# A hybrid decoder layer on one core: blocks of the delta rule's inverse turned by VectorE, side work in other slots, convolution states turned four tiles at a time

## The chip, the core and the metric

The kernel runs on one core of a Trainium2 chip. A core has TensorE (PE: matmuls and their weight loads), VectorE (DVE), ScalarE (ACT), GpSimd (POOL) and SyncE (SP, which here only issues DMAs). They run side by side and wait for each other through semaphores. The metric is the device time of one execution in microseconds (us). Of the kernel before, three runs were timed: 2022.98, 2025.06 and 2025.74 us, median 2025.06 us.

## The reference, cut to what matters

One layer for a prompt (256 tokens) and 8 samples of 8 tokens, 320 columns in all, in float32:

```python
h = rms_norm(x); proj = h @ w_in        # -> u (S5) | q k v | z | beta | a | two gates
# branch A: S5, a diagonal complex state space model, 64 groups, scan over positions
y = gelu(Re(C h) + D u);  y = y * sigmoid(y @ w_glu + b_glu)
# branch B: causal convolution (width 4) over [buf | qkv], SiLU, l2-norm of q and k, gated delta rule
out = sum_j xp[:, j:j + L] * w[j];  conv_new = xp[:, L:]        # the convolution states go in and out
lower = where(strict, beta * (k k^T) * decay, 0)                # one 128x128 matrix for each head and chunk
tmat = triangular_solve(eye + lower, eye)                       # the inverse
u = tmat @ (v * beta);  w = tmat @ (k * beta * exp(gc))
# merge, output projection, SwiGLU FFN (5632), a gated input embedding, final norm
x = x + (sigmoid(ga) * (y_s5 @ w_a) + sigmoid(gb) * (y_dn @ w_b)) @ w_out
x = x + (silu(h2 @ w_gate) * (h2 @ w_up)) @ w_down
x = x + (p @ w_ple) * sigmoid(h3 @ w_ple_gate)
```

## The kernel before

**Units.** All large products are cut into units. A unit is four tiles of 128 rows of a weight by 256 columns, loaded by SP into `raw` (a ring of four). ScalarE rounds it to `whi` (`split_hi`, L931), VectorE takes the rest `wlo = raw - whi` (`split_lo`, L1384), and TensorE multiplies in three parts of eight matmuls: `whi` with the high part of the activations, `whi` with the low part, `wlo` with the high part (L2117). Four units (two in `glu`, `wa`, `wb`) make a pair of output tiles in PSUM (`pg`), which VectorE takes out (`evac`).

**Slots.** `schedule()` writes the order of the mixer by hand: a list of slots, each with a list of side work and a number of units. Within a slot TensorE does its side work first and then the units; VectorE, ScalarE and POOL do the slot's units first (their splits and evacuations) and then its side work. Every engine runs through its own instructions strictly in this order. Side products land in two PSUM regions, `side_a` and `side_b`; `side_fills()` lists in which order they are filled. A region is filled again when the one before was drained.

**Stages of the mixer**, with the time in the profile: x turned and the first norm (to 50 us); set-up of the S5 tables, a long chain on POOL (33 to 93 us); sixteen S5 slots (88 to 308 us), in which TensorE makes the drives (`drive`, L2465) before the last unit of an odd slot and the readouts (`readout`, L2481 to L2490) before the last unit of an even one, while VectorE works through `s5_tiles`; the tail, in which the last three columns of the convolution go out (`tail`, L2276; `tailc`, L1704); eight convolution slots (`conv`, L1716) with the small decay functions (`decay`, L1072 to L1078) put between them; l2 norms (`l2a`, `l2s`, `l2b`); the delta rule in three chunks of 128, 128 and 64 columns (426 to 700 us); the gate products `glu` with `late` (L1460 to L1462), and then `wa` and `wb`.

**The inverse.** `per_block` (L2160) multiplies the 32x32 blocks on the diagonal of each head. `tm` holds the inverse so far, `tmt` its transpose; at level k TensorE makes `m1 = ltm . tm` (side work `m1`), ScalarE copies it out, then TensorE makes `ta = tmt . m1` and `tb = m1 . tmt` (`tab`), and VectorE subtracts `ta` from `tm` (L1828) and `tb` from `tmt` (L1837). At level 0 a product with the identity gives the transpose of `ltm` (`ident,ltm`). Levels 5 and 6 join the blocks to larger ones. Chunks 0 and 1 have seven levels, chunk 2 has three.

## Time and profile before

| what | value |
|---|---|
| median of three runs | 2025.06 us |
| the profiled execution's own time | 2022.08 us |
| its span, first to last instruction | 2020.3 us |
| PE busy | 1997.2 us (99%), 16379 matmuls |
| DVE busy | 1117.8 us (55%) |
| ACT busy | 822.8 us (41%) |
| POOL busy | 295.0 us (15%) |
| chain that ended last | PE 93%, DVE 3%, ACT 2%, issue 1% |
| DMA | 154 GB/s mean |

The page also cuts the span into 40 slices of 50 us and gives the busy share in tenths: in slices 3 to 6 (100 to 300 us, the S5 stage) DVE reads 9, 9, 9, 8 and ACT 4, 3, 3, 3; in slices 7 and 8 (the tail and the convolution stage) ACT reads 6 and 8. Busy time of PE is not PE at its peak, since matmuls are pipelined and their ends are modelled; the time from the start of one group to the start of the next tells more. "issue" is idle time for which the profile shows no releaser. A timeline row gives the start, the time, engine, line, operation, output<-inputs, the count of merged instructions, and in brackets the idle time before it with what ended it. A float32 matmul stands as two instructions in the trace where the program has one.

### The profile page before, as it was taken

To read this page: it belongs to the slowest core of one execution; us is meant where nothing else is said; L and a number is where in the kernel's file an instruction comes from. 1 tells how busy PE (TensorE), PEld (TensorE's weight loads), DVE (VectorE), ACT (ScalarE), POOL (GpSimd) and SP (SyncE) were. 2 spreads that over 40 slices of the span, in tenths; PEclk is the share of its full clock that TensorE was granted. 3 is DMA by queue.
4 is the path that set the end of the run, shared out by engine and by line. 5 is a ranking of instruction groups with operands and counts; after the bars stand their busy time and mean duration, and the time that the engine had idled before them with its cause. 6 is when DMAs were issued, how large, how long until landed. Compare 5 with 4: busy or idle time off the path is not lost.

```text
span 2020.3 us, 40308 instructions
## 1 busy us (share of the span) xinstructions
PE 1997.2 (99%) x16379; PEld 1952.0 (97%) x16379; DVE 1117.8 (55%) x1401; ACT 822.8 (41%) x1076; POOL 295.0 (15%) x372
## 2 busy tenths in 40 slices
PE   9999999999999999999999999999999999999998
PEld 8999999899999879999999999999999999999998
DVE  6899987674535677644444444333444444444554
ACT  7343336843433455343433333333333333334543
POOL 3855532000002110011000000000000000011110
PEclk9999999999999999999999999999999999999999
DMA  8544444544345686744444444444544444444442
GB/s 200 182 137 147 126 136 143 148 120 138 111 122 166 187 250 214 238 151 150 146 147 154 146 148 155 146 151 146 156 145 149 152 146 151 145 147 152 150 146 100
DMA packets 299648, 310.26 MB, mean 154 GB/s; under 512 B 24771, under 2 KB 290068, under 8 KB 299220
## 3 DMA queue, kind: packets, MB, share of 16 engines
q1 hardware_dynamic: 295844, 296.76, 47.9%
q0 software_dynamic: 3264, 11.64, 2.1%
q8 instruction: 91, 1.49, 0.3%
q14 instruction: 31, 0.25, 0.0%
q10 hardware_dynamic: 418, 0.12, 0.0%
HBM read 291.34 MB, written 17.14 MB: 153 GB/s over the span
## 4 chain that ended last, share of the span: by engine, by line
PE 93%; DVE 3%; ACT 2%; issue 1%; DMA 0%; SPq 0%; ACTq 0%; DVEq 0%
PE pg L2117 86%; DVE cacc L1716 1%; PE side_a L2160 1%; DVE wlo L1384 1%; PE side_a L2151 1%; ACT whi L931 1%; PE side_b L2160 0%; PE side_a L2465 0%; PE side_a L2117 0%; DMA xtok<-in_x_sample 0%; PE side_b L2124 0%; PE side_a L2484 0%; PE side_b L2426 0%; PE side_b L2117 0%; ACT qkv L1002 0%
## 5 line engine op out<-in xcount | busy, mean ns | idle before, releaser
L1384 DVE TENSOR_TENSOR wlo<-raw,whi 128x1024 fp32r<-128x1024 f32 (+1 forms) x528 | 651.3, 1241 | 660.0 <-ACT whi L931 658.4
L931 ACT ACTIVATE whi<-raw 128x1024 fp32r<-128x1024 f32 (+1 forms) x528 | 545.3, 1039 | 910.3 <-PE pg L2117 867.1
L2117 PE MATMUL pg<-xhi,whi 128*128 128x320 f32 x2816 | 479.4, 312 | 2.5 <-ACT whi L931 2.5
L2117 PE MATMUL pg<-xhi,wlo 128*128 128x320 f32 x2816 | 470.6, 309 | 1.3 <-issue 1.2
L2117 PE MATMUL pg<-xlo,whi 128*128 128x320 f32 x2816 | 470.2, 309 | 0.0
L2117 PEld LDWEIGHTS pg<-xhi,whi 128*128 128x128 f32 x2816 | 424.7, 188 | 13.0 <-issue 6.7
L2117 PEld LDWEIGHTS pg<-xhi,wlo 128*128 128x128 f32 x2816 | 427.3, 188 | 0.5 <-DVE wlo L1384 0.3
L2117 PEld LDWEIGHTS pg<-xlo,whi 128*128 128x128 f32 x2816 | 427.5, 188 | 0.0
L915 POOL TENSOR_TENSOR fsi<-fsg,inv 128x640 f32<-128x640 f32 x22 | 43.4, 1971 | 707.5 <-ACT fsg L1267 707.5
L2117 PE MATMUL pg<-mlo,whi 128*128 128x320 f32 x704 | 118.8, 309 | 0.0
L2117 PE MATMUL pg<-mhi,whi 128*128 128x320 f32 x704 | 118.8, 309 | 0.0
L2117 PE MATMUL pg<-mhi,wlo 128*128 128x320 f32 x704 | 118.8, 309 | 0.0
L2117 PEld LDWEIGHTS pg<-mhi,whi 128*128 128x128 f32 x704 | 107.4, 188 | 0.0
L2117 PEld LDWEIGHTS pg<-mlo,whi 128*128 128x128 f32 x704 | 107.4, 188 | 0.0
L2117 PEld LDWEIGHTS pg<-mhi,wlo 128*128 128x128 f32 x704 | 107.4, 188 | 0.0
L658 POOL TENSOR_TENSOR pt<-ta,tb 128x256 f32<-128x256 f32 x64 | 70.6, 1123 | 80.6 <-DVE gg L1608 79.2
L900 POOL TENSOR_TENSOR acc<-acc,sq 128x320 f32<-128x320 f32 x23 | 23.3, 1012 | 397.1 <-ACT sq L939 397.1
L2117 PE MATMUL pg<-mxhi,wlo 128*128 128x320 f32 x256 | 42.9, 309 | 0.0
L2117 PE MATMUL pg<-mxlo,whi 128*128 128x320 f32 x256 | 42.8, 309 | 0.0
L2117 PE MATMUL pg<-mxhi,whi 128*128 128x320 f32 x256 | 42.7, 309 | 0.0
L2117 PEld LDWEIGHTS pg<-mxhi,wlo 128*128 128x128 f32 x256 | 39.1, 188 | 0.0
L2117 PEld LDWEIGHTS pg<-mxhi,whi 128*128 128x128 f32 x256 | 38.9, 188 | 0.0
(491 smaller groups left out, 1700.8 us busy)
## 6 DMA issues: line engine op xcount, KB each, us to landing
raw<-in_w_in SPq DMA_DIRECT2D x144, 512.0 KB, 4.0
raw<-in_w_gate SPq DMA_DIRECT2D x88, 512.0 KB, 3.5
raw<-in_w_up SPq DMA_DIRECT2D x88, 512.0 KB, 3.5
raw<-in_w_down SPq DMA_DIRECT2D x80, 512.0 KB, 3.4
raw<-in_w_out SPq DMA_DIRECT2D x32, 512.0 KB, 3.4
raw<-in_w_ple_gate SPq DMA_DIRECT2D x32, 512.0 KB, 3.4
raw<-in_w_a SPq DMA_DIRECT2D x16, 512.0 KB, 5.5
raw<-in_w_b SPq DMA_DIRECT2D x16, 512.0 KB, 4.2
```

What stands on the lines that cost most here:

```text
L658: ins = pool.tensor_tensor(out, a, b, op)
L900: pool.tensor_tensor(acc[:], acc[:], sq[:, 0, :], ALU.add).then_inc(sem("pool_steps"), 1)
L915: pool.tensor_tensor(fsi[:], fsg[:], inv[:].unsqueeze(1).broadcast_to([P, 2, N]), ALU.mult).then_inc(sem("fsi_ready"), 1)
L931: act.activation(whi[:, r, 0:nk, :], raw[:, r, 0:nk, :], ACT.Copy).then_inc(w_hi, 1)
L1384: dve.tensor_tensor(wlo[:, r, 0:nk, :], raw[:, r, 0:nk, :], whi[:, r, 0:nk, :].bitcast(F32), ALU.subtract).then_inc(w_lo, 1)
L1716: ins = dve.scalar_tensor_tensor(out=s, in0=qkv[:, t, j:j + NCV], scalar=w, in1=s, op0=ALU.mult, op1=ALU.add)
L2117: ins = pe.matmul(out[:, m, 0:N], w[:, r, k, m * P:(m + 1) * P], a[:, k0 + k, :], start=first and k == 0 and part == 0, stop=last and k == ...
L2151: ins = pe.matmul(out[0:rows or P, h // 4, (h % 4) * n:(h % 4) * n + n], lhs(h), rhs(h), start=True, stop=True)
L2160: ins = pe.matmul(out[r, h // 4, (h % 4) * size:(h % 4 + 1) * size], lhs(h, r), rhs(h, r), start=True, stop=True)
```

## The change

The slots are written anew in places: one unit moves from S5 slot 3 to the tail slot, the second unit of `bmix` to `norm`, and `decay` moves from the convolution slots to S5 slots 1 to 5. `evac(0)` moves behind the first norm. The squares of the l2 norm go from ScalarE to VectorE. In the inverse the products `ident,ltm` and (at levels 1 to 4) `ta` go; `tm` is now made by VectorE as the blockwise transpose of `tmt` (`turn_blocks`), and TensorE waits for `tm_turned`. The second half of `dg` becomes `dgb`, one slot later. The convolution states are turned four tiles of channels at a time: 6 transposes of 96 or 108 rows in place of 24 of 24 or 27, with four DMAs in and eight out in place of one and two. x is loaded in three pieces of columns (512, 512, 1024) in place of two. The evacuation of the last `glu` pair moves ahead of the split of its unit.

```diff
-            order += [("a", ("m1", c, k))]
+            order += [("a", ("m1", c, k))] * (k > 0)
-            order += [("b", ("ta", c, k))] * (0 < k < LEVELS[c] - 1) + [("ab"[k == LEVELS[c] - 1], ("tb", c, k))] * (k > 0)
+            order += [("b", ("ta", c, k))] * (k == 5) + [("ab"[k == LEVELS[c] - 1], ("tb", c, k))] * (k > 0)
...
-    slot([("norm", 0)], 1)
-    slot([("bmix", 1), ("bmix", 0)], 1)
+    slot([("norm", 0)], 2)
+    slot([("bmix", 1), ("bmix", 0)], 0)
...
-        slot([("s5", hq)], 3 + (hq % 2 and hq > 1))
+        slot([("s5", hq)] + [("decay", hq - 1)] * (1 <= hq < 6), 3 + (hq % 2 and hq > 3))
...
-    slot([("tailc",), ("s5out",), ("tail",)], 1)
+    slot([("tailc",), ("s5out",), ("tail",)], 2)
...
+            def turn_blocks(n):
+                dve.transpose(tm[0:n].rearrange("p h j -> p (h j)"), tmt[0:n].rearrange("p h j -> p (h j)")).then_inc(sem("tm_turned"), 1)
...
-                    o.step(dve.tensor_tensor(tmt[0:n], eye, ltm[0:n], ALU.subtract))
-                    drain(dve.tensor_tensor(hsplit(tm[0:n]), hsplit(eye), blocks_of(key)[0:n], ALU.subtract), key)
-                    o.settle()
+                    o.link(dve.tensor_tensor(tmt[0:n], eye, ltm[0:n], ALU.subtract))
+                    turn_blocks(n)
...
                         drain(dve.tensor_tensor(hsplit(tmt[0:n]), hsplit(tmt[0:n]), blocks_of(kk)[0:n], ALU.subtract), kk)
+                        if k < LEVELS[c] - 1:
+                            wait_drained(dve, kk)
+                            turn_blocks(n)
...
-                    act.activation(sql[:, :, 0:NCV], qkv[:, t:t + 4, 0:NCV], ACT.Square).then_inc(sem("l2sq_ready"), 1)
+                    dve.tensor_tensor(sql[:, :, 0:NCV], v, v, ALU.mult).then_inc(sem("l2sq_ready"), 1)
...
-                    for j in range(3):
-                        key = ("tail", j)
-                        out = begin(key)
-                        for t in range(8):
-                            ins = pe.transpose(out[0:27, t // 4, (t % 4) * P:(t % 4 + 1) * P], tail[:, 8 * j + t, :], ident[:])
-                        end(ins, key)
+                    out = begin(key)
+                    for j in range(KC // 4):
+                        ins = pe.transpose(out[0:4 * 27, j // 3, (j % 3) * P:(j % 3 + 1) * P],
+                                           tail[:, 4 * j:4 * j + 4, :].rearrange("p t c -> p (t c)"), ident[:])
+                    end(ins, key)
...
-                    if j == last and last >= 3 and prev is not None:
+                    if j == last and last >= 3 and prev:
+                        evac(prev)
+                    if j == last and prev is not None and pairs[prev][0:2] == ("glu", 3):
                         evac(prev)
                     split_lo(n, n % RING, nk)
```

How the instructions stand in the rows of an engine's order, at three places. TensorE, chunk 0 of the delta rule, the first levels of the inverse, before:

```order
L2117 MATMUL pg<-xhi,wlo 128x320 x8
L2160 MATMUL side_a<-ident,ltm 32x32 x32
L2117 MATMUL pg<-xhi,whi 128x320 x8
L2117 MATMUL pg<-xlo,whi 128x320 x8
L2117 MATMUL pg<-xhi,wlo 128x320 x8
L2160 MATMUL side_a<-tm,ltm 32x32 x32
L2117 MATMUL pg<-xhi,whi 128x320 x8
L2117 MATMUL pg<-xlo,whi 128x320 x8
L2117 MATMUL pg<-xhi,wlo 128x320 x8
L2160 MATMUL side_b<-m_142,tmt 32x32 x32
L2160 MATMUL side_a<-tmt,m_142 32x32 x32
```

and now, from two units ahead of the first `tm,ltm`:

```order
L2133 MATMUL pg<-xhi,wlo 128x320 x8
L2133 MATMUL pg<-xhi,whi 128x320 x8
L2133 MATMUL pg<-xlo,whi 128x320 x8
L2133 MATMUL pg<-xhi,wlo 128x320 x8
L2176 MATMUL side_a<-tm,ltm 32x32 x32
L2133 MATMUL pg<-xhi,whi 128x320 x8
L2133 MATMUL pg<-xlo,whi 128x320 x8
L2133 MATMUL pg<-xhi,wlo 128x320 x8
L2176 MATMUL side_a<-tmt,m_143 32x32 x32
```

The group `ident,ltm` and, of the pair, the group in `side_b` are gone; the rest stands as before. VectorE, two levels of the same chunk, before:

```order
L1384 TENSOR_TENSOR wlo<-raw,whi 128x1024
L1624 TENSOR_TENSOR ltm<-lt,lvl 128x256
L1828 TENSOR_TENSOR tm<-tm,side_b 128x256
L1837 TENSOR_TENSOR tmt<-tmt,side_a 128x256
L1384 TENSOR_TENSOR wlo<-raw,whi 128x1024 x2
```

and now:

```order
L1382 TENSOR_TENSOR wlo<-raw,whi 128x1024
L1626 TENSOR_TENSOR ltm<-lt,lvl 128x256
L1847 TENSOR_TENSOR tmt<-tmt,side_a 128x256
L1621 STREAM_TRANSPOSE tm<-tmt 128x256
L1382 TENSOR_TENSOR wlo<-raw,whi 128x1024 x2
```

The subtraction into `tm` is replaced by a transpose that stands behind the one into `tmt`. VectorE around the tail (`yt` is the last readout taken in, `g` the evacuation of a gate pair, `cacc` the first convolution), before:

```order
L1384 TENSOR_TENSOR wlo<-raw,whi 128x1024
L1614 SCALAR_TENSOR_TENSOR yt<-yt,par_67,side_a 128x320
L1429 TENSOR_TENSOR g_131<-pg,inv 128x640
L1384 TENSOR_TENSOR wlo<-raw,whi 128x1024
L1704 COPY tail<-qkv 128x24x3
L1706 COPY tail<-qkv 128x24x24
L1384 TENSOR_TENSOR wlo<-raw,whi 128x1024 x2
```

and now:

```order
L1382 TENSOR_TENSOR wlo<-raw,whi 128x1024
L1612 SCALAR_TENSOR_TENSOR yt<-yt,par_67,side_a 128x320
L1382 TENSOR_TENSOR wlo<-raw,whi 128x1024
L1427 TENSOR_TENSOR g_132<-pg,inv 128x640
L1382 TENSOR_TENSOR wlo<-raw,whi 128x1024
L1707 COPY tail<-qkv 128x24x3
L1709 COPY tail<-qkv 128x24x24
L1382 TENSOR_TENSOR wlo<-raw,whi 128x1024 x2
```

One more `wlo` stands between the last readout and the copies into `tail`.

## Rows read from the trace of the kernel before

**Rows 1.** Who TensorE waited for: us in total, times, longest.

```profile
PE pg L2117 <- DVE glo L1462: 4.7, 1, 4.7
PE pg L2117 <- ACT whi L931: 2.5, 6, 0.8
...
PE pg L2117 <- issue: 1.2, 1, 1.2
PE side_a L2160 <- issue: 0.9, 1, 0.9
...
PE side_b L2283 <- ACT sql L1124: 0.6, 1, 0.6
```

**Rows 2.** Timeline of TensorE, chunk 0: start, us, line, names, count.

```profile
444.57 0.75 PE L2160 MATMUL side_a<-ident,ltm 32*32 32x32 f32 x64
445.26 1.44 PE L2117 MATMUL pg<-xhi,whi 128*128 128x320 f32 x8
...
453.37 0.72 PE L2160 MATMUL side_b<-m,tmt 32*32 32x32 f32 x62
...
454.61 1.44 PE L2117 MATMUL pg<-xhi,whi 128*128 128x320 f32 x8
...
458.33 0.75 PE L2160 MATMUL side_a<-tm,ltm 32*32 32x32 f32 x64
```

**Rows 3.** Timeline of VectorE, early set-up and chunk 0.

```profile
22.75 0.94 DVE L1502 RECIPROCAL sc<-sc 32x128 f32<-32x128 f32 x1
...
464.08 0.42 DVE L1837 TENSOR_TENSOR tmt<-tmt,side_a 128x256 f32<-128x256 f32 x1
```

**Rows 4.** Timeline of ScalarE, convolution stage.

```profile
362.55 1.28 ACT L1072 ACT_TABLE_LOAD   x1
```

**Rows 5.** Timeline of TensorE, convolution stage.

```profile
361.95 1.33 PE L2117 MATMUL pg<-xlo,whi 128*128 128x320 f32 x8
363.13 1.34 PE L2117 MATMUL pg<-xhi,wlo 128*128 128x320 f32 x8
365.25 1.40 PE L2117 MATMUL pg<-xhi,whi 128*128 128x320 f32 x8 [0.79 <-ACT whi L931]
```

**Rows 6.** Timeline of VectorE, tail and first convolution slot.

```profile
312.14 1.23 DVE L1384 TENSOR_TENSOR wlo<-raw,whi 128x1024 fp32r<-128x1024 f32 x1 [0.75 <-ACT whi L931]
...
313.43 0.46 DVE L1706 COPY tail<-qkv 128x576 f32<-128x576 f32 x1
...
323.01 4.73 DVE L1716 SCALAR_TENSOR_TENSOR cacc<-qkv,par,cacc 128x344 f32<-128x344 f32 x9
```

**Rows 7.** Timeline of TensorE, states turned: coming in, and the tail going out.

```profile
32.77 1.65 PE L2186 MATMUL side_a<-ident,csn 24*128 24x24 f32 x24
...
314.23 1.04 PE L2276 MATMUL side_a<-ident,tail 128*27 128x128 f32 x8
...
318.46 1.41 PE L2117 MATMUL pg<-xhi,whi 128*128 128x320 f32 x8
```

**Rows 8.** Timeline of VectorE, S5 stage.

```profile
92.75 0.89 DVE L1578 TENSOR_TENSOR tt<-uu,side_a 128x320 f32<-128x320 f32 x2 [0.18 <-POOL uu L791]
...
119.44 0.48 DVE L1589 TENSOR_TENSOR tt<-uu,side_a 128x320 f32<-128x320 f32 x1
...
134.67 0.54 DVE L1614 SCALAR_TENSOR_TENSOR yt<-yt,par,side_a 128x320 f32<-128x320 f32 x1
```

**Rows 9.** Timeline of TensorE, S5 stage.

```profile
121.12 0.47 PE L2481 MATMUL side_a<-yt,k 32*32 32x160 f32 x8
...
137.03 0.41 PE L2465 MATMUL side_a<-yt,bbt 32*128 32x160 f32 x2
```

**Rows 10.** Timeline of VectorE, last `glu` pair.

```profile
709.71 0.82 DVE L1460 TENSOR_TENSOR tg<-yt,g 128x640 f32<-128x640 f32 x1 [0.80 <-ACT g L984]
```

**Rows 11.** Timeline of TensorE, same place.

```profile
711.97 2.50 PE L2117 MATMUL pg<-ghi,whi 128*128 128x320 f32 x8 [4.75 <-DVE glo L1462]
```

**Rows 12.** Busy us by stretch: PE, PEld, DVE, ACT, POOL; granted clock, DMA.

```profile
709.70:716.50 6.80, 4.53 (x17) 4.53 (x18) 6.66 (x7) 6.80 (x17) 1.76 (x2) 0.50 0.73 203
```

More of the change, by code:

```diff
@@ L58 @@
 MASKED = [5, 5, 3]
+TURNS = [0, 5, 10]
 SB, HB = 32, 64
@@ L98, in side_fills @@
     order += [("a", ("y", K5 - 1)), ("b", ("hl",))]
-    order += [("ab"[j % 2], ("tail", j)) for j in range(3)]
+    order += [("a", ("tail",))]
     order += [("ba"[r % 2], ("l2s", r)) for r in range(4)]
@@ L186, in schedule @@
         slot([("dg", c)], 1)
-        slot([("dkv", c)], 1)
+        slot([("dgb", c), ("dkv", c)], 1)
         slot([("dkk", c)], 1)
         for k in range(LEVELS[c]):
-            slot([("m1", c, k)] + [("ks", 1)] * (c == 1 and k == 6), 1)
+            slot([("m1", c, k) if k else ("t0", c)] + [("ks", 1)] * (c == 1 and k == 6), 1)
             if k:
@@ L405, in hybrid_layer @@
         tail = zt2.take("tail", [P, KC, 3 + 3 * NB])
-        ttok = zt2.take("ttok", [27, CCH])
+        ttok = zt2.take("ttok", [4 * 27, KC // 4, P])
         zst = Zone(nc, zq_at, 4 * 4096)
@@ L853, in _ @@
                     elif what == "tail":
-                        for j in range(3):
-                            wait_drained(pool, ("tail", j))
-                        pool.dma_start(conv_prompt[0, 0], ttok[0:3, :]).then_inc(sem("tail_stored"), 16)
-                        pool.dma_start(conv_sample[0].rearrange("b j c -> (b j) c"), ttok[3:27, :]).then_inc(sem("tail_stored"), 16)
+                        wait_drained(pool, key)
+                        for t in range(4):
+                            pool.dma_start(by_quads(conv_prompt[0, 0])[:, :, t], ttok[27 * t:27 * t + 3]).then_inc(sem("tail_stored"), 16)
+                            pool.dma_start(by_quads(conv_sample[0].rearrange("b j c -> (b j) c"))[:, :, t],
+                                           ttok[27 * t + 3:27 * t + 27]).then_inc(sem("tail_stored"), 16)
                     elif what == "s5out":
@@ L1022, in side @@
                         act.wait_ge(sem("row_squares"), c)
-                    for h in range(2):
+                    for h in range(3):
                         act.wait_ge(sem(f"x_landed_{h}"), 48)
@@ L1103, in side @@
                     first_taps(0)
-                    for j in range(3):
-                        wait_filled(act, ("tail", j))
-                        drain(copy(ttok[:, j * 1024:(j + 1) * 1024].rearrange("p (k c) -> p k c", k=2),
-                                   ps(("tail", j))[0:27, :, :]), ("tail", j))
+                    wait_filled(act, key)
+                    drain(copy(ttok[:].rearrange("p (k j) c -> p k (j c)", k=2), ps(key)[0:4 * 27, :, 0:3 * P]), key)
                 elif what == "conv":
@@ L1154, in side @@
                     drain(act.activation(hsplit(vb[0:n]), ps(("vt", c))[0:n].rearrange("p k (h c) -> p k h c", h=4), ACT.Copy), ("vt", c))
-                elif what == "m1" and a[1]:
+                elif what == "m1":
                     c, k = a
@@ L2181, in side @@
                 elif what == "cst":
-                    pe.wait_ge(sem("csn_landed"), 16)
+                    pe.wait_ge(sem("csn_landed"), 16 * 4)
                     out = begin(key)
-                    for t in range(KC):
-                        c = (t % 12) * 3 * NB
-                        ins = pe.transpose(out[:, t // 12, c:c + 3 * NB], csn[:, t * P:(t + 1) * P], ident[0:3 * NB, 0:3 * NB])
+                    for j in range(KC // 4):
+                        c = (j % 3) * 4 * 3 * NB
+                        ins = pe.transpose(out[:, j // 3, c:c + 4 * 3 * NB], csn[:, j, :], ident[0:4 * 3 * NB, 0:4 * 3 * NB])
                     end(ins, key)
                 elif what == "x":
-                    if a[0] % 4 == 0:
-                        pe.wait_ge(sem(f"x_landed_{a[0] // 4}"), 48)
+                    if a[0] in (0, 2, 4):
+                        pe.wait_ge(sem(f"x_landed_{a[0] // 2}"), 48)
                     out = begin(key)
```

74 lines of the change are left out of this document (39 added, 35 removed).

## The prediction

> **What bounds the kernel now.** I read the waits of TensorE first, since it is busy nearly the whole span, and then its timeline around each place that the change touches, start to start: matmuls are pipelined, so the time from the start of one group to the start of the next is what a group costs. TensorE waits for very little: 4.7 us once for VectorE's `glo`, 2.5 us in six pieces for ScalarE's `whi`, 0.6 us for ScalarE's squares `sql`, and a gap of 1.2 us that nothing in the profile explains [rows 1]. So a matmul that is taken out of TensorE's queue comes off the span one for one, and work added to another engine costs only where it is later than TensorE. A weight unit is three groups of eight matmuls of 320 columns at 1.17 us each (361.95 to 363.13) [rows 5], 3.52 us; with side work at both ends it takes 3.72 us (454.61 to 458.33) [rows 2]. So a group of side matmuls costs its own time and about 0.2 us for the joints. I work from the profiled execution: span 2020.3 us, its own time 2022.08 us, 1.8 us around the span. The median of the timed runs is 2025.06 us, 3.0 above it; I take the gain from the trace off the median, and a little more off since single runs of this kernel differ by nearly 3 us.
>
> **Delta rule's inverse: instructions removed.** The first product of each chunk, `ident,ltm`, is 32 blocks (64 in the trace) and lasts 444.57 to 445.26, 0.69 us [rows 2]; with the two joints it is 0.87 us for chunks 0 and 1, and about 0.81 for the small chunk 2: 2.55 us for three. A pair `tb` and `ta` lasts 453.37 to 454.61, 1.24 us; one of the two alone is as long as the `ident,ltm` group, 0.69, so dropping `ta` saves 0.55. It goes at four levels in chunks 0 and 1 (8 times) and once in chunk 2 (I take 0.5): 4.9 us. Together **7.5 us**, and this part is certain if nothing becomes late.
>
> What could become late is the turn by VectorE. After the change a subtraction into `tmt`, then the transpose of 128x256, stand between the end of the pair and the next `tm,ltm`. TensorE reaches that 3.72 us after the end of the pair (454.61 to 458.33) [rows 2]; VectorE's subtraction into `tmt` starts 0.1 us after the pair is filled and lasts 0.42 us [rows 3], and the subtraction into `tm` that stood before it is gone. That leaves about 3.1 us for the transpose. The trace of before has no transpose on VectorE. From below it is bounded by the plain subtraction of the same 128x256, 0.42 us; a copy may be cheaper, but no cheaper turn changes anything. From above by the dearest VectorE row per column, the reciprocal, 0.94 us for 128 columns, so 1.9 us for 256 [rows 3]. I take 0.5 us; both ends lie inside 3.1 us, so the turn costs nothing, and VectorE's total stays level, since each turn replaces one subtraction. Behind the turn on VectorE is the next `wlo` (1.2 us), which TensorE needs only at the third part of its unit.
>
> The Trainium skill ("VectorE: DVE Perf Modes", section "The three transpose paths") says that VectorE turns 32x32 blocks on their own, 311 ns for 128x128 in bf16. Its fp32 formula for a tensor_tensor, in the section on the TRN2 errata, would give an estimate of 0.42 us for 256 columns, as the subtraction row has it. By that price the turn is hidden too. The same page speaks against more instructions on VectorE, since each pays a fixed latency; the two orders have as many, so it would not change the sum.
>
> **Unexplained gaps.** TensorE's waits list 1.2 us inside a unit and a second gap near it, inside a pair, 0.9 us [rows 1]; I count 2.5 us for both with the slower matmuls around them. Both are in chunk 1, where TensorE runs through small instructions fastest (a pair is 64 instructions in 1.24 us, where a unit has 24 in 3.5). I read them as TensorE's instructions arriving late. With two fifths of the small ones gone, I take off **2.0 us** of 2.5; the bounds are 0 (they only move) and 2.5.
>
> **Convolution stage: ScalarE's function tables.** Before the change the side work `decay` stands in the conv slots and brings a switch of tables: 1.28 us for the table, two tiny functions, the next `whi`, and then the table back [rows 4]. Beside such a slot TensorE's next unit starts 2.12 us after 363.13 instead of 1.17, for ScalarE's `whi` [rows 5]. That is the first of four such delays up to 386 us (0.95, 0.46, 1.0 and 0.8 us start to start; the list of waits counts most of them in its 2.5). The decay goes into the S5 slots, where ScalarE is three to four tenths busy by the page's slices. Then VectorE is the next to be late: a conv slot costs it 4.7 us for nine taps, two `wlo` of 1.15 and half a gate, about 7.3 [rows 6] against TensorE's 7.04, so eight slots eat 2 us of its lead. The second unit of the tail slot gives it 3.5 us of lead more. I take all of it: **3.2 us**, bounds 1.5 and 3.2. The squares `sql` go from ScalarE to VectorE. VectorE is not behind there, a square of 1376 columns should take about 1.6 us by the 1.2 us of `wlo` for 1024, and TensorE comes 3.6 us after the sums it waits for; the waits for `sql` (0.6, and two smaller) go: **0.7 us**.
>
> **Tail and incoming convolution states.** The outgoing tail takes 314.23 to 318.46, 4.23 us [rows 7], for 24 transposes of 0.11 us each, 2.6 us; the rest is waiting for ScalarE's `ttok`. Six transposes are 0.65 us. But VectorE now has two units before the copies `tail`. Before, the one `wlo` started at 312.14 and the copies ended at 313.9, 0.3 us ahead of TensorE [rows 6, 7]. Now one `wlo` more and the gate's evacuation lie between, about 1.9 us. I work it out to a wait of 1.7 us ahead of the six transposes: 4.2 - 1.7 - 0.7 = **1.8 us**, bounds 1.0 and 3.5. The incoming states take 1.65 us for 24 transposes [rows 7]; six are 0.65, so 1.0 us, but see the next part. Six more output DMAs on POOL, some 0.55 us each, stand before nothing: VectorE wants them 90 us later.
>
> **S5 stage: gains before it are taken away.** The S5 tiles hang on a chain of POOL and VectorE: VectorE waits for POOL's `uu` at 92.75 and not again until 140 us [rows 8]. TensorE is close behind: its readout at 121.12 needs the drive that VectorE drains at 119.92, 1.2 us of room, and the drive at 137.03 needs `yt` of 135.21, 1.8 us [rows 8, 9]. The change takes one unit out of slot 3, so TensorE comes 3.5 us earlier to that drive; VectorE is spared one `wlo` and the two evacuations of a pair there, 2.2 us, and has 0.3 us of decay more. Before S5 TensorE wins 1.0 us by the six transposes and 0.4 by the second unit beside the norm. At 121 us it may come only 0.9 us earlier; at the drive room is 1.8 - 0.3 - (3.5 - 2.2) = 0.2 us. So of 1.4 us won before, **0.2 us** survive, and a new wait of about 1 us in all appears between 105 and 135 us. The start may come 0.5 us earlier with x in three pieces, as TensorE's warm-up ends 0.5 us before x lands; I take 0.3 of it, so **0.5 us** for both. Unit order after the tail is as before. POOL's chain runs beside a VectorE whose order changes, and how much that moves it no row says; I take -2 and +2 as bounds.
>
> **End of the gate products.** TensorE idles 4.75 us for `glo` [rows 11], and from 709.7 to 716.5 us the granted clock is 0.50, that is 1.2 GHz [rows 12]; the first part after it takes 2.5 us instead of 1.3. The last evacuation now stands ahead of `wlo`, so ScalarE's sigmoid runs beside `wlo` and the 0.80 us wait goes [rows 10]. **0.8 us**; bounds 0.5 and 2.9, the upper if the clock stays up. After an idle of 4 us I expect it to fall still.
>
> **Sum.** 7.5 + 2.0 + 3.2 + 0.7 + 1.8 + 0.5 + 0.8 = 16.5 us. The profiled execution would come to 2022.1 - 16.5 = 2005.6 us, the median to 2025.1 - 16.5 = 2008.6; I say **2008 us**.
>
> **Rivals.**
> - *Slower.* The turn is on TensorE's path. Nine turns (four, four, one) have 3.1 us of room each. To eat 16.5 us they must be late by 1.8 us each, so a turn must last over 5.0 us; at 5.5 us the kernel is at 2025.1 - 16.5 + 9 x 2.4 = 2030 us. Against it: the dearest row gives 1.9 us. 2 in 100.
> - *The waits move, they don't go.* VectorE takes ScalarE's place in the conv stage (its slot is longer than TensorE's), and the unexplained gaps come elsewhere. Then only removed instructions count: 7.5 + 1.8 + 0.5, about 10 us, 2015 us. For it: VectorE's 7.3 against 7.04; against it: the 3.5 us of new lead. 15 in 100.
> - *More than that.* POOL's chain is quicker, the tail doesn't wait and the clock stays up: 1.5 + 1.7 + 2 more, 21 to 22 us, 2003 us. 15 in 100.
> - *Absorbed altogether*: S5 loses 2 us or more and DMA landings late in chunk 2 and the wide stages take the rest; within 0.2% (4 us), which is about what can be told from no change here. Against it: TensorE waits for no DMA behind S5. 3 in 100.
> - The forecast has the rest, 65 in 100, with 2005 to 2012 as its own range.
>
> Eight in ten: 2003 to 2015 us. Faster 0.95, same 0.03, slower 0.02.
>
> **What would show it.** In the new profile: a transpose row under 1 us and no wait of TensorE for it; the pair groups 0.69 us long; no wait for `whi` between 320 and 400 us; a new TensorE wait of 1 to 2 us ahead of `tail`, and small ones for VectorE between 105 and 135 us; the idle before `ghi` near 4 us. I am wrong if a wait for `wlo` shows in the conv stage, or if S5 costs more than it did.

## The result, and the profile after

The changed kernel takes 2005.4 us, median of four runs (2003.9 to 2006.4), against 2024.8 us (2023.0 to 2025.7): the ratio is 0.9908, with a 95% interval of 0.9892 to 0.9924. A second set of four runs gave 2006.1 us and 0.991 (0.9894 to 0.9927). So it is faster by 18 us, give or take 3. The forecast was 2008 us, in a range of 2003 to 2015. The profiled execution has a span of 2004.6 us, 15.7 us less than before; the profiled execution of before ran 2.7 us under its median (2022.1 against 2024.8) and that of the changed kernel 0.9 over its own (2006.3 against 2005.4), which is why the medians are further apart than the traces.

Who TensorE waited for in the changed kernel (us in total, times, longest):

```profile
PE pg L2133 <- DVE glo L1460: 3.8, 1, 3.8
PE side_b L2195 <- DMA par2n<-in_conv_w: 2.0, 1, 2.0
PE side_b L2191 <- POOL ident L674: 1.7, 1, 1.7
PE side_a L2290 <- DVE tail L1709: 1.5, 1, 1.5
...
PE side_a L2478 <- issue: 0.9, 1, 0.9
PE side_a L2494 <- DVE tt L1587: 0.7, 1, 0.7
PE side_a L2478 <- DVE tt L1587: 0.6, 1, 0.6
PE pg L2133 <- ACT whi L937: 0.5, 1, 0.5
```

Set beside [rows 1]: the waits for `whi` in the convolution stage, for `sql`, and both unexplained gaps of the delta rule are gone; `glo` is 0.9 us less. New are 2.0 us for a load at the start, 1.5 us ahead of `tail`, and 2.1 us in three pieces at the S5 drives and a readout (109, 122 and 135 us); the third, put to "issue", ends 0.1 us after VectorE's `yt` is written.

Adding up waits isn't enough, since matmuls that are gone stand in no list. I laid the traces side by side by the start of the same groups. The one unit that moved from the S5 stage to the tail slot is put right with its 3.52 us.

| stretch | before | after | gain |
|---|---|---|---|
| start to the S5 parameters' transposes (`ident,sc`) | 31.62 | 32.67 | -1.05 |
| from there to `hl`, one unit put right | 278.43 | 279.15 | -0.72 |
| `hl` to the unit behind `tail` | 4.89 | 2.96 | 1.93 |
| from there to the first `sql`, one unit put right | 66.90 | 63.53 | 3.37 |
| to the first `gcr` | 41.56 | 40.83 | 0.73 |
| delta rule, to the first unit with `ghi` | 275.46 | 264.93 | 10.53 |
| to the first unit with `mxhi` | 131.44 | 131.24 | 0.20 |
| from there to the last matmul | 1180.45 | 1180.08 | 0.37 |

The sum is 15.4 us; the other 0.4 us are behind the last matmul. Not every row is exact to its decimals: among traces that have the same code there, the row to `mxhi` lies between 130.6 and 132.1 us and the last one between 1178.5 and 1180.5, so the last two gains are within the spread. The rows from `hl` to the first unit with `ghi` repeat within 0.1 us in traces of the same code, but for the inverse of before: with its unexplained gaps it takes 275.46 us here and 274.00 in states_only.

The inverse in the changed kernel, timeline of TensorE, and then of VectorE:

```profile
456.70 0.75 PE L2176 MATMUL side_a<-tmt,m 32*32 32x32 f32 x64
457.39 1.43 PE L2133 MATMUL pg<-xhi,whi 128*128 128x320 f32 x8
...
461.10 0.75 PE L2176 MATMUL side_a<-tm,ltm 32*32 32x32 f32 x64
```

```profile
450.36 0.45 DVE L1621 STREAM_TRANSPOSE tm<-tmt 128x256 f32<-128x256 f32 x1
...
457.50 0.42 DVE L1847 TENSOR_TENSOR tmt<-tmt,side_a 128x256 f32<-128x256 f32 x1 [1.47 <-PE side_a L2176]
457.96 0.45 DVE L1621 STREAM_TRANSPOSE tm<-tmt 128x256 f32<-128x256 f32 x1
458.32 1.18 DVE L1382 TENSOR_TENSOR wlo<-raw,whi 128x1024 fp32r<-128x1024 f32 x1
```

A pair's group and the joint behind it last 0.69 us now (456.70 to 457.39) where the pair took 1.24 [rows 2]. The turn takes 0.45 us and is done at 458.4; TensorE comes for `tm` at 461.10.

The tail, TensorE:

```profile
312.26 0.38 PE L2283 MATMUL side_b<-ident,hl 128*128 128x128 f32 x2
314.15 0.87 PE L2290 MATMUL side_a<-ident,tail 128*108 128x128 f32 x6 [1.52 <-DVE tail L1709]
314.78 1.42 PE L2133 MATMUL pg<-xhi,whi 128*128 128x320 f32 x8
```

Six transposes take 0.62 us, but TensorE stands idle for 1.52 us in front of them, where before it went straight on [rows 7].

### The profile page after: what moved, and what is told of

It is laid out like the page before. It is cut to its first block, busy times and chain, and to the rows that moved or that the text cites. A ratio compares the mean times of both kernels' runs of the same rounds, so it can differ in the third digit from the quotient of the medians.

```text
span 2004.6 us, 38837 instructions
## 1 busy us (share of the span) xinstructions
PE 1984.6 (99%) x15639; PEld 1941.8 (97%) x15639; DVE 1123.7 (56%) x1405; ACT 813.6 (41%) x1068; POOL 299.1 (15%) x378
## 4 chain that ended last, share of the span: by engine, by line
PE 93%; POOL 3%; DVE 2%; DMA 1%; issue 1%; ACT 0%; ACTq 0%; SPq 0%; DVEq 0%; POOLq 0%
PE pg L2133 86%; POOL sc5w L664 1%; POOL pt L664 1%; PE side_a L2176 1%; PE side_a L2167 1%; DMA raw<-in_w_out 1%; DVE wlo L1382 1%; PE side_a L2133 0%; PE side_a L2478 0%; DMA par2n<-in_conv_w 0%; DVE gg L1576 0%; PE side_a L2497 0%; PE side_b L2439 0%; PE side_b L2133 0%; PE side_b L2140 0%
```

## Experiments

Times are medians of four runs (three timed rounds and the profiled one; eight where said), each beside runs of the kernel before, 2023.4 to 2024.0 us. Four runs of one kernel lie within 1.5 to 4.3 us of each other, so for a microsecond or two the traces' stretches decide, not the medians.

**turn_only.** The kernel before with the turn alone:

```diff
-            order += [("a", ("m1", c, k))]
+            order += [("a", ("m1", c, k))] * (k > 0)
...
-                    drain(dve.tensor_tensor(hsplit(tm[0:n]), hsplit(eye), blocks_of(key)[0:n], ALU.subtract), key)
+                    turn_blocks(n)
```

> The kernel before with one part of the change: VectorE turns the blocks of the inverse, and TensorE's products `ident,ltm` and `ta` (levels 1 to 4) are gone. Nothing else moves. If instructions that leave TensorE's queue come off one for one and the turn is hidden: 7.6 us for the groups (0.87, 0.87, 0.81 and nine times 0.55 to 0.6), and the two unexplained gaps of 1.2 and 0.9 us with their surroundings go too, 2.5 us: 10 us off, 2014 to 2015 us, and no wait for the transpose. Rival: the gaps belong to TensorE's instruction fetch in that stretch and only move: then 7.6 us, 2017 us, with issue gaps of about 1 us elsewhere in chunk 0 or 1.

Measured: 2012.3 us, ratio 0.994 (0.9924 to 0.9957), 2 us less than I expected. The delta rule's stretch is 265.25 us, 10.2 less than before, and between 430 and 700 us the list of TensorE's waits is empty: no transpose, no unexplained gap. So the turn alone gives what the whole change has there (10.5). That the gaps hang on the number of small instructions is only partly shown: in `states_only`, below, the inverse is as before, and one gap of 1.0 us stood there in place of 1.2 and 0.9, and the stretch was 274.0 us, not 275.5. The ten traces in which each turn is made once have 264.9 to 265.3 us.

**decay_back**, `decay` in the convolution slots again, and **unit14**, the tail slot's second unit in S5 slot 14:

```diff
-        slot([("s5", hq)] + [("decay", hq - 1)] * (1 <= hq < 6), 3 + (hq % 2 and hq > 3))
+        slot([("s5", hq)], 3 + (hq % 2 and hq > 3))
...
-        slot([("conv", h)], 2)
+        slot([("decay", 0)] * (h == 4) + [("conv", h)] + [("decay", h - 4)] * (h > 4), 2)
```

```diff
-        slot([("s5", hq)] + [("decay", hq - 1)] * (1 <= hq < 6), 3 + (hq % 2 and hq > 3))
+        slot([("s5", hq)] + [("decay", hq - 1)] * (1 <= hq < 6), 3 + (hq % 2 and hq > 3) + (hq == 14))
...
-    slot([("tailc",), ("s5out",), ("tail",)], 2)
+    slot([("tailc",), ("s5out",), ("tail",)], 1)
```

> The changed kernel with `decay` back in the convolution slots. Theory: ScalarE's table loads there held up `whi` by 3.2 us, and `decay` costs VectorE 0.6 us in S5 slot 1 ahead of the readout. So the conv stage gets 3 to 3.5 us longer, with TensorE's waits for `whi` of up to 0.8 us back at 365 to 386 us, and the time ahead of the tail gets 0.6 us shorter: 2.6 us more in all, 2008 us. Rival: the conv stage's waits went because VectorE and ScalarE have one more unit of lead from the tail slot; then the waits stay away, and the kernel gains the 0.6 us, 2005 us.

> The changed kernel with the second unit of the tail slot put into S5 slot 14. Theory: the 1.5 us wait ahead of the transposes of `tail` goes, since VectorE has one `wlo` and one evacuation less ahead of the copies, and VectorE's lead is used up in the conv stage: up to 1 us of waiting for `wlo` comes back at 360 to 400 us. In all 0.5 to 1.5 us faster, 2004.5 us. Rival: VectorE needs that unit of lead; a conv slot takes it 7.3 us against TensorE's 7.04, and without the lead it is late by 2 us or more in the conv stage: 2006 us or slower.

Measured: decay_back 2004.4 us (2003.2 to 2004.9), not slower than the changed kernel. The convolution stretch is 63.54 us, as in the changed kernel (63.53), and no wait for `whi` stands in it, though ScalarE loads its tables there as before. My theory failed here: moving `decay` away was not what ended the `whi` waits. unit14: 2005.4 us. The wait ahead of `tail` is gone (from `hl` to the unit behind it 1.23 us instead of 2.96), and the convolution stretch is 64.56 us, 1.03 more, so 1.0 of the 1.7 us won is lost behind it. The list of waits shows no wait between 316 and 390 us, the one for `wlo` that I expected neither: the microsecond is in nine small slips, of 0.07 to 0.23 us from start to start. About 0.7 us of it is at the first groups of units, which need ScalarE's `whi`, and the rest at one `wlo` and one `sql` of VectorE.

**decay_back_unit14**, both edits together.

> The changed kernel with two parts undone together: `decay` back in the convolution slots, and one unit in the tail slot (the other goes to S5 slot 14). Each alone left the convolution stage nearly as it is in the changed kernel (67.1 us from the first unit behind the tail to `sql` with `decay` back; 1.0 us more with the unit moved). Theory: the four delays for `whi` of the kernel before (3.2 us) need both, a ScalarE that is held up by table loads and a tail slot with one unit; then they come back here, 64.6 + 2.3 to 3.4 us, that is about 67 us from the first unit behind the tail to `sql` (one unit less in it), and the kernel takes 2.5 us more than with `decay` back alone, 2007 us. Rival: what held up ScalarE before was the three copies of `ttok` in the tail slot, of which the changed kernel has one; then the stage stays at 63.5 to 64.6 us and the time at 2004.5 us.

Measured: 2007.5 us (2005.7 to 2008.2), 3.2 us more than decay_back. The stretch is 67.89 us, and the waits in it (320 to 420 us) are those of before again:

```profile
PE pg L2133 <- ACT whi L937: 3.0, 3, 1.9
PE side_b L2298 <- DVE sql L1730: 0.3, 1, 0.3
```

ScalarE at the first of them, and TensorE:

```profile
358.61 1.53 ACT L940 ACTIVATE cacc<-qkv,par 128x344 f32<-128x344 f32 x3
360.16 1.28 ACT L1078 ACT_TABLE_LOAD   x1
361.45 0.21 ACT L1078 ACTIVATE gab<-gab 128x8 f32<-128x8 f32 x1
...
361.68 1.99 ACT L937 ACTIVATE whi<-raw 128x1024 fp32r<-128x1024 f32 x2
```

```profile
359.60 1.33 PE L2133 MATMUL pg<-xhi,wlo 128*128 128x320 f32 x8
362.86 1.41 PE L2133 MATMUL pg<-xhi,whi 128*128 128x320 f32 x8 [1.93 <-ACT whi L937]
```

The delay needs both: a ScalarE held up by a table load, and a tail slot with one unit, after which VectorE and ScalarE run close ahead of TensorE. Moving `decay` alone takes away all but 1.0 us of it (unit14), the second unit alone all of it (decay_back). The rival (the three copies of `ttok`) is out: this kernel has one, and the waits are there.

**states_only.** The kernel before with the states turned four tiles at a time, one unit in the tail slot, `decay` as before.

```diff
-                        for t in range(8):
-                            ins = pe.transpose(out[0:27, t // 4, (t % 4) * P:(t % 4 + 1) * P], tail[:, 8 * j + t, :], ident[:])
+                        ins = pe.transpose(out[0:4 * 27, j // 3, (j % 3) * P:(j % 3 + 1) * P],
+                                           tail[:, 4 * j:4 * j + 4, :].rearrange("p t c -> p (t c)"), ident[:])
```

> The kernel before with one part of the change: the convolution states turned four tiles at a time, coming in and going out (6 transposes in place of 24, one copy of `ttok` in place of three, more DMAs), and nothing else; the tail slot keeps one unit and `decay` stays in the convolution slots. Theory: TensorE's tail goes from 4.23 us to about 1 us, since VectorE has its copies ready 0.3 us ahead as before, and the incoming states from 1.65 to 0.5 us. If that leaves the `whi` delays of the convolution stage as they are (66.9 us from the first unit behind the tail to `sql`), the gain is 3.3 + 0 to 1.1 us: 2020 us. Rival: the two copies that ScalarE no longer makes end the `whi` delays as well; then the stage is 63.5 us long and the gain is about 7 us: 2017 us.

Measured: 2018.3 us (eight runs, 2015.9 to 2020.5), ratio 0.9971 (0.996 to 0.9982). From `hl` to the unit behind the tail 1.23 us instead of 4.89, a gain of 3.66. But the convolution stretch is 68.17 us, 1.27 longer: TensorE comes 3.7 us earlier to the same splits, and one wait for `whi` is 1.9 us where the longest was 0.8. The incoming states' 1.1 us are lost on the spot to a new wait for `wlo` (1.0 us, up to 45.5 us). The trace also gained 1.5 us in the delta rule and 1.0 behind it, where nothing was changed.

```profile
PE pg L2122 <- ACT whi L938: 3.6, 6, 1.9
...
PE pg L2122 <- DVE wlo L1389: 1.0, 1, 1.0
PE side_a L2165 <- issue: 1.0, 1, 1.0
```

So the second unit in the tail slot (1.5 us of waiting ahead of `tail`) is the price for not having 1.3 us and more behind it.

**par_split**, **x_two** and **after_again**, on the start. par_split waits for `par1n` alone and turns `par2n` with the S5 parameters; x_two loads x in two pieces; after_again is the changed kernel unaltered.

```diff
-                    pe.wait_ge(sem("par_landed"), 16 * 8)
+                    pe.wait_ge(sem("par_landed"), 16 * 7)
```

```diff
-            for h, cols in enumerate((slice(0, D // 4), slice(D // 4, D // 2), slice(D // 2, D))):
+            for h in range(2):
+                cols = slice(h * (D // 2), (h + 1) * (D // 2))
```

> The changed kernel, but TensorE's transpose of the norm weights waits only for `par1n`; the convolution weights `par2n` are loaded after the S5 parameters and turned with `s5par`. Theory: in the changed kernel TensorE idles 1.95 us at 9.1 us for `par2n`, the granted clock falls to 0.5 from about 11.7 to 18.3 us, and POOL's chain starts 1.05 us later than before, which the whole S5 stage passes on. Without that wait (it shrinks to about 0.6 us, since `par1n` lands a little earlier) POOL's chain starts at 32.7 us or earlier instead of 33.76, and TensorE reaches the tail 1 to 1.5 us earlier: 2004.2 us. Rival: the S5 stage is late by the slot that lost a unit and by `decay`, and POOL's chain follows its own start only in part; then under 0.4 us of it arrives at the tail.

> The changed kernel with x loaded in two pieces of 1024 columns again. In the traces the first unit starts at 15.72 us (before), 16.50 (before with the turn alone), 16.35, 14.62 and 16.63 (changed kernel and two variants with the same loading), and TensorE waits for `par2n` between 0.2 and 1.95 us in these. Theory: three pieces gain nothing since TensorE needs `par` in any case, which lands at about 10.6 to 11.1 us; with two pieces the first unit stands between 15.7 and 16.6 us and the kernel is within 1 us of the changed one, 2004.5 to 2006.5 us. Rival: the small pieces are what delays `par2n`; then two pieces are faster by 1 us or so, first unit at 15.5 us or earlier every time.

> The changed kernel once more, unaltered, for the spread of its start. In six traces so far the first unit started at 14.62 to 16.63 us, by when the weights of the norm landed and whether the granted clock fell to 0.5 around 12 to 18 us; kernels with the same code up to there are among them. Theory: this is spread from one execution to the next, and the loss of 1.8 us ahead of the tail that the first trace of the changed kernel showed against the kernel before is for a part such spread: the start differs again by 0.5 us or more from 16.35, and the end of POOL's chain (94.01 us) with it, one for one, while the 60.2 us from that chain's start to its end stay. Rival: the start is a property of the kernel, and it comes within 0.3 us of 16.35 again.

Measured: par_split 2005.7 us, x_two 2005.5 us, after_again 2006.1 us. No difference from the changed kernel in the medians. The traces tell more. Eight traces share the changed kernel's code up to the first unit, and that unit starts at 14.62, 14.65, 14.71 and 14.83 us in four of them, at 16.35, 16.63, 16.81 and 16.93 us in the others. In all eight the transpose of `par1n` starts at 10.6 to 11.4 us; what differs is what stands before and behind it. In the late four TensorE has had x early, waits 1.6 to 2.0 us for `par2n`, and the granted clock is 0.5, that is 1.2 GHz and not 2.4, for 6.8 us from 11.5 to 12.4 us on. In three of the early four it waits 0.2 us for it at most, and the clock stays at 1.0; in the fourth it waits 0.65 and the clock is 0.5 from 13.5 to 16.9 us. The late kind (the changed kernel), TensorE:

```profile
11.06 0.29 PE L2195 MATMUL side_b<-ident,par1n 81*128 81x81 f32 x1 [1.95 <-DMA par2n<-in_conv_w]
...
12.80 1.90 PE L2140 MATMUL side_b<-ident,xtok 128*128 128x128 f32 x6
```

and its stretches (columns as in [rows 12]), behind them those of the early kind (decay_back):

```profile
12.00:14.00 2.00, 2.00 (x8) 1.11 (x8) 1.52 (x4) 2.00 (x5) 0.00 (x0) 0.50 1.05 364
14.00:16.00 2.00, 2.00 (x9) 1.56 (x9) 1.63 (x3) 2.00 (x5) 0.00 (x0) 0.50 1.14 187
```

```profile
12.00:14.00 2.00, 2.00 (x12) 1.30 (x12) 1.94 (x4) 2.00 (x5) 0.00 (x0) 1.00 1.08 345
14.00:16.00 2.00, 2.00 (x17) 2.00 (x17) 1.62 (x3) 2.00 (x6) 0.00 (x0) 1.00 1.13 175
```

With x in two pieces the first unit started at 15.72, 16.50 and 16.54 us (before and its two variants) and in x_two at 16.07. The mean of the four is 16.2 us, that of the eight with three pieces 15.7 (14.7 for the early four, 16.7 for the late four), which is no more than single traces of one code differ by. The piece that lands first doesn't bring the work forward where `par` is what TensorE waits for, until 10.6 to 11.4 us in seven of the eight; it makes the idle in front of `par` longer. The late start is not a matter of three pieces alone: turn_only and states_only have x in two, wait 1.1 us for x and 0.5 us for `xt`, and have the 6.8 us at 0.5 too.

x_two is as its theory had it, in one trace. par_split started at 14.68, its POOL chain at 32.52 us instead of 33.76, and it reached the tail 1.24 us earlier; behind the gate products the trace gave 0.8 of it back. Its theory is not shown by this: the unaltered code reaches 14.6 in some traces, the medians don't differ, and the clock fell in par_split too (0.5 from 13.7 to 17.2 us) though no wait for `par2n` was left. after_again did not settle the rival alone (16.81 against 16.35, chain start 34.12 against 33.76), but with the other seven traces it does: the start is spread.

What the start loses goes through the S5 stage whole, since that follows POOL. Seven other traces have the changed kernel's S5 slots, one with a unit more (unit14). Their `ident,sc` starts at 30.0 to 33.3 us, and the stretch from there to `hl`, that unit put right, is 279.2 to 279.3 us in six of them (279.15 in the changed kernel); glu_back has 279.86, with a wait of 0.5 us for `wlo` at 102 us. In the changed kernel, POOL and VectorE:

```profile
33.76 1.10 POOL L664 TENSOR_TENSOR sc5w<-sp 128x32 f32<-128x32 f32 x3 [31.05 <-ACT sp L940]
...
93.72 0.29 POOL L797 COPY uu<-uu 128x128 f32<-128x128 f32 x1
```

```profile
94.04 0.89 DVE L1576 TENSOR_TENSOR tt<-uu,side_a 128x320 f32<-128x320 f32 x2 [2.26 <-POOL uu L797]
...
114.42 0.18 DVE L1680 TENSOR_TENSOR ba<-ba,gab 128x24 f32<-128x24 f32 x1
114.64 0.49 DVE L1681 SCALAR_TENSOR_TENSOR sp<-ba 128x24 f32<-128x24 f32 x1
```

The chain takes 60.2 us (60.0 before), and VectorE's first S5 tile starts at 94.04 us, 1.29 later than in [rows 8]. `decay` puts 0.6 us on VectorE ahead of the readout at 121.94. But that is not what the S5 stage mainly lost by. In decay_back the wait at that readout is gone and the next one, at the drive for `yt`, is 1.18 us instead of 0.86: the stretch is 278.88 us (278.89 in decay_back_unit14), 0.3 less. In best2, which has the fourth unit in slot 3 again, that drive has no wait, and the stretch is 277.75 us, another 1.1 less.

**turn_x6** and **turn_x12**: each turn six or twelve times, each waiting for the one before.

```diff
+                for _ in range(5):
+                    o.link(dve.transpose(tm[0:n].rearrange("p h j -> p (h j)"), tmt[0:n].rearrange("p h j -> p (h j)")))
                 dve.transpose(tm[0:n].rearrange("p h j -> p (h j)"), tmt[0:n].rearrange("p h j -> p (h j)")).then_inc(sem("tm_turned"), 1)
```

> The changed kernel with each of the twelve turns of `tm` done six times in a row, each waiting for the one before. A turn takes 0.445 us, and in chunk 0 it starts at 457.96 us where TensorE comes for `tm` at 461.10: room for 3.1 us. Theory (prediction's slack): six turns take about 2.9 us, so nothing changes at levels 1 to 4; behind the first turn of a chunk (441.0 us, TensorE at 443.5) it is late by 0.4 us, three times: 1 us more, 2006.5 us. Rival: VectorE's `wlo` behind the turn is what TensorE runs into, since 29 us more of VectorE work stand in the stretch where it was five tenths busy; then 3 us or more are lost, and the waits name `wlo`.

> The same with each turn twelve times: about 5.8 us where there is room for 3.1, so TensorE waits some 2.7 us (3.3 behind the first turn of a chunk) each of twelve times: 33 us more than the changed kernel, 2038 us, and the changed kernel is slower than the one before. That is the prediction's rival with its turning point. Rival: other waits hide part of it (TensorE's own joints, VectorE catching up in the unit slots): then 15 to 25 us.

Measured: 2012.6 us and 2053.4 us, 7 and 48 us more than the changed kernel, where I expected 1 and 33. The stretch of the delta rule is 271.28 and 313.50 us, 6.3 and 48.6 more. In turn_x6 TensorE waits 5.6 us in six pieces: behind the first turn of chunks 0 and 1 (0.6 and 1.0, where I expected 0.4), for `wlo` behind that (0.5 twice, the rival in small), and at a place that I had missed, the turn at the end of level 1 (1.9 and 1.2). turn_x6, VectorE, and TensorE:

```profile
448.46 1.21 DVE L1827 TENSOR_TENSOR eg<-eg,qt 128x1024 f32<-128x1024 f32 x1
449.60 1.21 DVE L1829 TENSOR_TENSOR ktok<-ktok,dl 128x1024 f32<-128x1024 f32 x1
...
453.38 2.36 DVE L1622 STREAM_TRANSPOSE tm<-tmt 128x256 f32<-128x256 f32 x5
455.77 0.45 DVE L1623 STREAM_TRANSPOSE tm<-tmt 128x256 f32<-128x256 f32 x1
```

```profile
456.32 0.74 PE L2178 MATMUL side_a<-tm,ltm 32*32 32x32 f32 x64 [1.89 <-issue]
```

VectorE has `eg` and `ktok` to do there and is behind. In the changed kernel that turn starts at 450.36 us with TensorE at 452.31, 1.95 us of room and not 3.1. (The profile puts the 1.89 us to "issue"; TensorE starts 0.1 us after the last turn's end, so it is that wait.)

In turn_x12 the waits are as I expected, twelve of them and 33.4 us in all. Its waits of TensorE from 430 to 720 us, and a stretch of it beside the same stretch of the changed kernel:

```profile
PE side_a L2178 <- issue: 19.6, 7, 4.1
PE side_a L2178 <- DVE ltm L1628: 8.6, 3, 3.8
PE side_a L2178 <- DVE tm L1623: 5.1, 2, 2.6
```

```profile
430.00:690.00 260.00, 226.62 (x2798) 217.45 (x2797) 170.51 (x309) 81.17 (x120) 10.94 (x19) 0.93 0.40 115
430.00:690.00 260.00, 260.00 (x3261) 247.28 (x3260) 142.13 (x218) 106.57 (x164) 15.87 (x28) 1.00 0.50 148
```

What I had left out is the clock. Among these idles it was granted at 0.5 for 34.1 us of the stretch, where it is 1.0 throughout in turn_x6 and in the changed kernel; matmuls at half the clock for that long account for at most 17 us, and 15.2 us is what is left of the 48.6 beside the waits.

With six turns (2.8 us together) the kernel is 11 us faster than the one before, with twelve (5.7 us, at 0.48 each) it is 30 us slower. Drawn straight between these, the change gains nothing at a turn of about 3.6 us; by the waits alone, one microsecond more in each of twelve turns being 12 us, it would be 4.4. No run stands between, so the turning point is an estimate of 3.6 to 4.4 us.

**glu_back.** VectorE's evacuation of the last `glu` pair behind the split again.

```diff
-                    if j == last and prev is not None and pairs[prev][0:2] == ("glu", 3):
-                        evac(prev)
```

> The changed kernel with VectorE's evacuation of the last `glu` pair behind the split of its unit again. Theory: `wlo` (1.2 us) and ScalarE's sigmoid (0.8 us of VectorE waiting) stand one behind the other again, TensorE idles 4.7 us instead of 3.8 for `glo`: 0.9 us more, 2006.3 us, with the same stretch of granted clock 0.5 behind the idle. Rival: the clock comes back later by as much as the idle is longer; then 1.5 us or more.

Measured: 2006.3 us; the wait for `glo` is 4.75 us instead of 3.84, as the theory had it, with the clock at 0.5 for 6.8 us as in the changed kernel. Whether 0.9 us is what the kernel loses is not shown. The stretch from the first `ghi` unit to `mxhi` is 132.53 us against 131.24 in the changed kernel, but the seven traces with the evacuation ahead and the same 6.8 us at 0.5 have 131.1 to 132.1, and the medians can't tell it either.

**best2**, put together from these: par_split, `decay` back in the convolution slots, four units in S5 slot 3 and three in slot 15, the transposes of `tail` in the slot behind their copies, and `late` for the last `glu` pair ahead of the split.

```diff
-        slot([("s5", hq)] + [("decay", hq - 1)] * (1 <= hq < 6), 3 + (hq % 2 and hq > 3))
+        slot([("s5", hq)], 3 + (hq % 2 and 1 < hq < 15))
...
-    slot([("tailc",), ("s5out",), ("tail",)], 2)
+    slot([("tailc",), ("s5out",)], 2)
...
-        slot([("conv", h)], 2)
+        slot([("tail",)] * (h == 0) + [("decay", 0)] * (h == 4) + [("conv", h)] + [("decay", h - 4)] * (h > 4), 2)
```

> A version from the findings: the changed kernel with `par1n` waited for alone, `decay` in the convolution slots, four units in S5 slot 3 and three in slot 15, the transposes of `tail` one slot later than the copies they wait for, and the last `glu` pair finished by VectorE ahead of its split. Expected against the changed kernel: 1.3 us at the start, about 1.5 us of waits in the S5 stage (107 to 135 us), 1.5 us ahead of `tail`, 1.2 us ahead of `glo`: 5 us, 2000.5 us. If S5 slot 15 with three units makes TensorE wait for the last readout, up to 2 us of it are lost. Rival: VectorE and ScalarE are what the stretch from 90 us to the tail follows, and the waits only move: then 2.5 us, 2003 us.

Measured: 2002.2 us (2001.6 to 2003.1), ratio to before 0.9898 (0.9881 to 0.9914). None of its four runs is as slow as any of the eight of the changed kernel (2003.9 to 2007.0): about 3.5 us faster, between the 5 us that I expected and the rival's 2.5. Against decay_back (2004.4 us), whose edit it contains, it is 2.1 us. Its waits:

```profile
PE pg L2132 <- DVE glo L1460: 3.6, 1, 3.6
...
PE pg L2132 <- ACT whi L937: 0.9, 2, 0.6
...
PE side_a L2478 <- DVE tt L1587: 0.6, 1, 0.6
```

The wait ahead of `tail` and two of the three S5 waits are gone. The stretch to `hl` is 277.75 us, 1.4 less. The convolution stage takes 1.0 us back, with waits of 0.3 us for `whi` (374 us) and for `sql` in it; I put that to less lead ahead of TensorE there, which no run tests. Finishing `glu` ahead of the split gave 0.2 us of 1.2: VectorE now stands idle 0.8 us for the sigmoid, which the split had filled.

## Why the prediction was right, and where it was not

The forecast held (2008 us, measured 2005.4 and 2006.1). By its own terms, forecast and what the traces show:

- *Instructions removed from the inverse and the gaps*, 7.5 + 2.0 us: 10.5, and 10.2 with the turn alone. The groups' prices came out as read from the rows; the gaps went altogether, and about 0.5 us more than both.
- *The turn is hidden*: yes, at 0.45 us. There are twelve turns (five, five, two) and not nine, since the first of each chunk counts too, and the room of 3.1 us holds from level 2 on: it is 1.95 us at the end of level 1. I read it at one level and took it nine times, and left out that TensorE's clock falls among the longer of such waits (turn_x12). That made the rival's point of return 5.0 us, where the experiments put it between 3.6 and 4.4.
- *Convolution stage*, 3.2: 3.4. The cause was half right. The fourth of the four delays that I added up, 0.8 us ahead of 385.36, is TensorE's wait for `sql` ([rows 1], 0.6) and not for `whi`; I then took it again with the squares. From start to start, the delays for `whi` are 2.7 us of the stretch and that wait 0.7, which the change ended too. The table loads did delay `whi`, but the second unit in the tail slot alone would have ended that. Two edits with nearly the same effect were made; the prediction named the lead as what keeps VectorE from being late, not as a cure of its own. Without it 1.0 us comes back (unit14), most of it at units that need ScalarE's `whi`.
- *Squares on VectorE*, 0.7: 0.7 behind the first `sql`, at 1.59 us each as estimated, beside the 0.7 ahead of it that stands in the item above. So the term was half of what it should have been, and the sum of both items, 4.1 us against 3.9, came out because the one had too much of what the other lacked. The stretch from the first `sql` to `gcr` is 40.83 us in all traces with the squares on VectorE, and 41.56 or 41.57 in the three without.
- *Tail*, 1.8: 1.9, with the wait of 1.5 us in its place.
- *End of the gate products*, 0.8: the wait is 0.9 shorter, with the clock falling still; the stretch is only 0.2 shorter, with a new wait of 0.5 us for `whi` at its end (818.83), and such differences are within its spread.
- *S5 stage and start*, +0.5: -1.8. This is the step that failed. I had three pieces of x gain 0.3 us and the S5 stage take back all but 0.2 of what is won before it. In the trace the start lost 1.05 us, and the S5 stage lost 0.7 us more. The first is spread, not the change: the same code starts its first unit at 14.6 or 16.9 us. I looked at what waits for x and not at what TensorE needs next, the weights of the norm, for which it waited until 10.6 us or later. The second is the change. TensorE wins 1.7 us from `ident,sc` to the first drive (85.80 and 86.46 us) and loses 2.4 behind it, 2.1 of that in the three waits where I had about 1. The mechanism was as I described it, the size was not: the rooms of 1.2 and 0.2 us were read off for two places and no room was worked out for the drive at 109 us (0.56). Of the loss 0.3 us is `decay` (decay_back); the wait that is left then, 1.18 us, goes with the fourth unit back in slot 3 (best2, which beside that and decay_back's edit has nothing new on the way to that drive except at the start).

The traces' gain is 15.7 us and the forecast's sum was 16.5. That they are so near is in part luck: the inverse gave 1.0 us more than its terms and the start and S5 stage 2.3 us less, 1.05 of it by a start that differs from one execution to the next. The medians' 18 is more than 15.7, since the trace of before, the base of every sum, ran 2.7 us under its median and the new one 0.9 over it; its first unit, for one, started 0.8 us earlier than in two other traces with that start. The unit beside the first norm, the order of its evacuation, `dgb` and the squares were not undone alone, so what each of them gives is read from the stretches only. The rival in which waits only move (2015 us) is out in the main, but its mechanism is there in small: states_only lost 1.3 us of 3.7 to it, unit14 1.0 of 1.7.

## What to carry to other kernels

On a kernel where one engine is busy 99% of the span, an instruction taken off that engine pays in full where nothing behind it is late: all of it in the inverse here, nothing of the 1.1 us of the incoming states in states_only. The same edit that frees the engine moves it closer to its suppliers; look behind each place where it comes earlier for what is next late, before counting the gain. Room for a new step is to be read at every place where it stands, not at the easiest one. And where two edits might end the same wait, undo each alone and both together: undone alone, one showed nothing here and the other 1.0 us, together they showed 4.4. And when a wait grows in an experiment, look at the clock behind it before putting the whole loss to the wait.

## What the runs showed of the hardware

- The clock at the start, in all fourteen traces. TensorE's idles between 7 and 12 us came to 0.5, 0.5 and 0.6 us in the three in which the granted clock stayed at 1.0; to 0.65, 0.7, 0.9, 1.0 and 1.15 us in the five in which it was 0.5 for 3.4 us, from 13.3 to 13.7 us on; and to 1.6 to 2.0 us in the six in which it was 0.5 for 6.8 us, from 11.5 to 12.6 us on. Between the early and the late kind of the changed code the first unit starts 2 us apart.
- Behind the idle of 3.6 to 3.8 us for `glo` the clock was 0.5 for 3.4 us in decay_back, x_two and best2, and for 6.8 us in the other traces with that idle; from the first `ghi` unit to `mxhi` the three took 130.6 us, the others 131.1 to 132.1.
- In turn_x12, among twelve idles of 1.3 to 4.1 us within 230 us the clock was at 0.5 for 34.1 us, in eight pieces of 3.4 or 6.8 us.
- The clock also fell without an idle. turn_only, TensorE, and the busy time and clock of two stretches of it:

```profile
34.18 1.64 PE L2190 MATMUL side_a<-ident,csn 24*128 24x24 f32 x24
35.75 2.25 PE L2121 MATMUL pg<-xhi,whi 128*128 128x320 f32 x8
37.80 2.09 PE L2121 MATMUL pg<-xlo,whi 128*128 128x320 f32 x8
39.73 1.33 PE L2121 MATMUL pg<-xhi,wlo 128*128 128x320 f32 x8
```

```profile
37.00:38.00 1.00, 1.00 (x5) 1.00 (x5) 0.93 (x3) 1.00 (x2) 1.00 (x3) 0.50 0.36 121
38.00:39.00 1.00, 1.00 (x6) 1.00 (x5) 0.97 (x2) 1.00 (x1) 0.92 (x2) 0.50 0.00 0
```

  Behind the 24 small transposes the two groups take 2.05 and 1.93 us, start to start, where 1.27 and 1.17 are usual. In the kernel before, the same transposes [rows 7] were followed by full speed.
- A 128x256 float32 transpose of 32x32 blocks on VectorE takes 0.445 us, about as long as a plain subtraction of that size (0.42); five in a row, each waiting for the one before, take 2.36 us.
